# Feed-forward up projections as seven block products of sums, with the split of h behind them

## The reference, cut to what matters

```python
def swiglu(x, w_in, w_out):
    g, u = jnp.split(x @ w_in, 2, axis=-1)
    return (jax.nn.silu(g) * u) @ w_out

h = h + 0.5 * swiglu(rms_norm(h, ffn1_norm[i]), ffn1_w_in[i], ffn1_w_out[i])
```

## Time and profile before

| what | value |
| --- | --- |
| median of 3 runs | 2918.87 us (2911.94 to 2919.1) |
| the profiled execution, its own time | 2917.88 us |
| its span | 2916.1 us |
| PE busy | 2889.1 us, 99% |
| DVE, ACT, POOL busy | 39%, 38%, 44% |
| DMA | 267.5 MB, mean 92 GB/s |
| weights of the up parts | 220 units of 512 KB |

### The profile page before, as it was taken

The page is one execution under the profiler, slowest core; times in us unless marked ns, Lnnn a source line. Parts: engine busy times, 40 slices in busy tenths (PEclk is TensorE's granted clock), DMA queues, the critical chain, the costliest instruction groups (busy, mean ns, idle before and its releaser), DMA issues.

```text
span 2916.1 us, 36136 instructions
## 1 busy us (share of the span) xinstructions
PE 2889.1 (99%) x13036; PEld 2328.5 (80%) x13036; DVE 1122.8 (39%) x1659; ACT 1094.7 (38%) x1508; POOL 1285.4 (44%) x588
## 2 busy tenths in 40 slices
PE   8999999999999999999999999999999999999999
PEld 7888877888888888888888886765688888788887
DVE  4223157322312221135322216579788363432210
ACT  4232266333323322243323333556444344432321
POOL 4444444444444444443444443158632363244443
PEclk9999999999999999999999999999999999999999
DMA  4323322333333333332333322112222352233332
GB/s 153 100 90 104 96 87 80 101 94 93 94 101 94 101 98 91 99 110 87 94 101 102 92 89 87 52 51 65 87 73 66 94 150 68 65 94 101 94 93 80
DMA packets 80653, 267.50 MB, mean 92 GB/s; under 512 B 11168, under 2 KB 13216, under 8 KB 80560
## 3 DMA queue, kind: packets, MB, share of 16 engines
q1 hardware_dynamic: 77904, 262.01, 30.0%
q10 hardware_dynamic: 2656, 4.26, 0.5%
HBM read 263.09 MB, written 2.10 MB: 91 GB/s over the span
## 4 chain that ended last, share of the span: by engine, by line
PE 94%; DVE 3%; issue 1%; ACT 1%; POOL 0%; DMA 0%; ACTq 0%; SPq 0%; DVEq 0%; POOLq 0%
PE bank L437 28%; PE bank L439 27%; PE bank L438 27%; PE bank L509 1%; PE bank L511 1%; PE bank L510 1%; PE bank L2414 1%; PE bank L1142 1%; PE bank L1554 1%; PE bank L2152 0%; PE bank L1563 0%; PE bank L2132 0%; PE bank L1214 0%; PE bank L736 0%; DVE hq L2323 0%
## 5 line engine op out<-in xcount | busy, mean ns | idle before, releaser
L420 POOL TENSOR_TENSOR w_lo<-w_stage,w_hi 128x1024 fp32r<-128x1024 f32 (+1 forms) x448 | 1059.0, 2366 | 1408.0 <-ACT w_hi L394 1402.7
L437 PE MATMUL bank<-xg_hi,w_hi 128*128 128x512 f32 x2384 | 942.0, 395 | 1.6 <-POOL w_lo L432 1.2
L439 PE MATMUL bank<-xg_hi,w_lo 128*128 128x512 f32 x2384 | 928.3, 389 | 0.0
L438 PE MATMUL bank<-xg_lo,w_hi 128*128 128x512 f32 x2384 | 928.3, 389 | 0.0
L394 ACT ACTIVATE w_hi<-w_stage 128x1024 fp32r<-128x1024 f32 (+2 forms) x500 | 515.4, 1033 | 530.2 <-PE bank L439 487.5
L437 PEld LDWEIGHTS bank<-xg_hi,w_hi 128*128 128x128 f32 x2384 | 447.5, 188 | 122.8 <-issue 29.6
L438 PEld LDWEIGHTS bank<-xg_lo,w_hi 128*128 128x128 f32 x2384 | 447.7, 188 | 94.9 <-issue 4.1
L439 PEld LDWEIGHTS bank<-xg_hi,w_lo 128*128 128x128 f32 x2384 | 447.5, 188 | 94.3
L438 PE MATMUL bank<-h_lo,w_hi 128*128 128x512 f32 x880 | 342.3, 389 | 0.0
L437 PE MATMUL bank<-h_hi,w_hi 128*128 128x512 f32 x880 | 342.3, 389 | 0.0
L439 PE MATMUL bank<-h_hi,w_lo 128*128 128x512 f32 x880 | 342.3, 389 | 0.0
(11 more groups left out here) (474 smaller groups left out, 2995.5 us busy)
## 6 DMA issues: line engine op xcount, KB each, us to landing
w_stage<-w_up SPq DMA_DIRECT2D x220, 512.0 KB, 3.5
w_stage<-w_down SPq DMA_DIRECT2D x80, 512.0 KB, 3.5
w_stage<-merge SPq DMA_DIRECT2D x36, 512.0 KB, 3.6
w_stage<-w_down SPq DMA_DIRECT2D x40, 384.0 KB, 3.1
w_stage<-hg_qfg SPq DMA_DIRECT2D x12, 512.0 KB, 3.5
w_stage<-rec_r SPq DMA_DIRECT2D x8, 512.0 KB, 3.6
w_stage<-rec_y SPq DMA_DIRECT2D x8, 512.0 KB, 3.5
w_stage<-rec_out SPq DMA_DIRECT2D x8, 512.0 KB, 3.5
```

Source lines behind the costliest of these rows:

```text
L420: pool.tensor_tensor(w_lo[:, r, 0:w], w_stage[:, r, 0:w], f32(w_hi[:, r, 0:w]), ALU.subtract).then_inc(w_lo_ready, 1)
L437: pe.matmul(out, w_hi[:, r, c], hi, start=start, stop=False)
L438: pe.matmul(out, w_hi[:, r, c], lo, start=False, stop=False)
L439: return pe.matmul(out, w_lo[:, r, c], hi, start=False, stop=stop)
```

## The change

In each up projection, the first and the last body (four pairs) stay as they were on PE. The 18 pairs between are computed by blocks. The pair's two units are the rows of a 2 x 2 block matrix (W11, W12 in the unit of u, W21, W22 in the unit of g; the columns are the first and the second four tiles of x), and x is a 2 x 2 block matrix too (four tiles by 256 tokens). Seven products of blocks, each of 4 x 3 matmuls of 128 x 256, take the place of eight.

This needs sums. Once per part, DVE makes four sums of blocks of x (13 operations, `x_sums`), ACT their high and POOL their low parts (`x_high`, `x_low`). For each pair, ACT copies W21 into PSUM, DVE makes S1, S2 and S4 there, POOL makes S3; ACT writes the four high parts, DVE three low parts and POOL one. After the products, ACT copies M1, and DVE adds the blocks into the banks of u and g (five additions of 256 columns and one of 512). The banks 4 and 5 hold M5, M6 and M7, the banks 6 and 7 the sums of W.

The gate is handled in a new way: DVE multiplies g by `rstd` (`take_gate`), ACT takes silu, POOL multiplies the result by `rstd` (`scale_gate`), and DVE multiplies it with u straight from PSUM into `h_raw` (`product`). h is split only after the loop (`high` on ACT, `low` on DVE), because its place in memory holds the sums of x until then. SyncE's loads in the loop also wait for S4 of the pair that held the place before. Semaphores that are free by then are used twice, under new names.

The core of the diff:

```diff
+    xsum = place("xsum", [P, 4, 2, 4, HALF], F32R, at=work + 64)
+    s1_w = place("s1_w", [P, 2, T], F32R, at=work + 33 * KB)
+    s2_w = place("s2_w", [P, 2, T], F32R, at=work + 37 * KB)
+    u_add0 = place("u_add0", [P, T], at=work + 41 * KB)
+    u3 = place("u3", [P, HALF], at=work + 43 * KB)
+    xsum_f = place("xsum_f", [P, 5, 4, HALF], at=work + 68 * KB)
...
+            for k in range(4):
+                c = slice(k * P, (k + 1) * P)
+                pe.matmul(out, wh[:, c], xh[:, k, :], start=k == 0, stop=False)
+                pe.matmul(out, wh[:, c], xl[:, k, :], start=False, stop=False)
+                mm = pe.matmul(out, wl[:, c], xh[:, k, :], start=False, stop=k == 3)
+            return mm
...
+        def step(b, p):
+            n = pair_at(b, p)
+            pe.wait_ge(w_lo_ready, n * 2 + (U.base + 5))
+            pe.wait_ge(taken, n * 2 + (U.rbase + 1))
+            product(right(g_bank(p)), w_block(p, 0, 0), x_block(0, 0)).then_inc(block_mm, 1)
+            pe.wait_ge(taken, n * 2 + (U.rbase + 2))
+            product(left(u_bank(p)), w_block(p, 0, 1), x_block(1, 0)).then_inc(unit_used, 1)
+            pe.wait_ge(wsum_lo_ready, after_wsum_lo(i, "S1", n))
+            if first_pair(n):
+                pe.wait_ge(std_ready, q + 1)
+                pe.wait_ge(pool_lo_ready, after_pool_lo(i, 0) - 1)
+            else:
+                pe.wait_ge(block_add, n * 5 + (after_add(i, "g2", 0) - 5))
+            product(M5_OUT, (s1_w[:, 0], s1_w[:, 1]), x_sum(0)).then_inc(block_mm, 1)
+            pe.wait_ge(w_lo_ready, n * 2 + (U.base + 6))
+            pe.wait_ge(block_copied, n + (PAIRS * i + 1))
+            product(left(g_bank(p)), w_block(p, 1, 1), x_sum(3))
+            pe.wait_ge(pool_lo_ready, after_pool_lo(i, n))
+            product(M7_OUT, (s3_w[:, 0], s3_w[:, 1]), x_sum(2)).then_inc(block_mm, 1)
+            pe.wait_ge(wsum_lo_ready, after_wsum_lo(i, "S2", n))
+            product(M6_OUT, (s2_w[:, 0], s2_w[:, 1]), x_sum(1)).then_inc(block_mm, 1)
+            product(right(u_bank(p)), w_block(p, 1, 0), x_block(1, 1)).then_inc(unit_used, 1)
...
+        for u in range(RING):
+            project_unit(pe, U, U.bodies - 1, u, xg_hi, xg_lo, free=U.rbase + 4 * (U.bodies - 1) - 2 + 2 * (u // 2))
         def down(b):
             for m in range(4):
-                pe.wait_ge(taken, b * 4 + (L.rbase + m + 1 - RING))
+                pe.wait_ge(taken, b * 4 + (L.rbase + (m | 1) + 1 - RING))
                 for part in range(3):
                     u = 3 * m + part
                     k1 = min(8 * part + 8, KF)
                     pe.wait_ge(w_lo_ready, b * L.per + (L.base + u + 1))
-                    pe.wait_ge(h_lo_ready, KF * i + k1)
                     for k in range(8 * part, k1):
+                        if m == 0:
+                            pe.wait_ge(h_lo_ready, KF * i + k + 1)
                         mm = three_passes(pe, bank[m][:], u % RING, k - 8 * part, h_hi[:, k, :], h_lo[:, k, :],
                                           k == 0, k == KF - 1)
                     mm.then_inc(unit_used, 1)
...
+        def x_low(t):
+            pool.wait_ge(wsum_hi_ready, (4 * PAIRS + 8) * i + 4 + t + 1)
+            pool.tensor_tensor(xsum[:, t, 1], xsum_f[:, 1 + t], f32(xsum[:, t, 0]), ALU.subtract).then_inc(pool_lo_ready, 1)
...
+        def scale_gate(j):
+            pool.wait_ge(silu_done, j + (KF * i + 1))
+            pool.tensor_tensor(gbuf[:], gbuf[:], rstd[:], ALU.mult).then_inc(silu_scaled, 1)
+        def step(b, p):
+            n, b1, p1 = pair_at(b, p), b + p, 1 - p
+            row(b1, p1, 0)
+            scale_gate(n + 1)
+            s3(n + 1, p1)
+            row(b1, p1, 1)
+            s3_low(n + 1)
+        for u in range(RING):
+            plain(0, u)
+        x_low(0)
+        x_low(1)
+        s3(0, 0)
+        row(1, 0, 0)
+        x_low(2)
+        x_low(3)
+        row(1, 0, 1)
+        scale_gate(0)
+        s3_low(0)
...
+        step(last - 1, 0)
+        plain(last, 0)
+        scale_gate(KF - 4)
+        plain(last, 1)
+        plain(last, 2)
+        scale_gate(KF - 3)
+        plain(last, 3)
+        scale_gate(KF - 2)
+        scale_gate(KF - 1)
...
+        def wsum_high(name, n, p):
+            dst = {"S1": s1_w[:, 0], "S2": s2_w[:, 0], "S3": s3_w[:, 0], "S4": w_hi[:, 2 * p + 1, 0:T]}[name]
+            src = {"S1": S12_BANK, "S2": S12_BANK, "S3": s3_f, "S4": S4_BANK}[name]
+            if name == "S3":
+                act.wait_ge(s3_done, n + (PAIRS * i + 1))
+            else:
+                act.wait_ge(wsum_done, after_wsum(i, name, n))
+            if name != "S4" and not first_pair(n):
+                act.wait_ge(block_mm, n * 4 + (after_block(i, {"S1": "M5", "S2": "M6", "S3": "M7"}[name], 0) - 4))
+            act.activation(dst, src[:], ACT.Copy).then_inc(wsum_hi_ready, 1)
...
+        def step(b, p):
+            n, b1, p1 = pair_at(b, p), b + p, 1 - p
+            copy21(b1, p1, n + 1)
+            copy_m1(n, p)
+            row1(b1, p1)
+            silu(n + 1)
+            wsum_high("S1", n + 1, p1)
+            row2(b1, p1)
+            wsum_high("S4", n + 1, p1)
+            wsum_high("S3", n + 1, p1)
+            wsum_high("S2", n + 1, p1)
...
+        for k in range(4):
+            act.activation(xsum_f[:, 0, k, :], x[:, k, 0:HALF], ACT.Copy, scale=col(*gain(k))).then_inc(wsum_hi_ready, 1)
+        x_high(0)
+        x_high(1)
+        copy21(1, 0, 0)
+        row1(1, 0)
+        x_high(2)
+        x_high(3)
+        wsum_high("S1", 0, 0)
+        row2(1, 0)
+        silu(0)
+        for name in ("S4", "S3", "S2"):
+            wsum_high(name, 0, 0)
+        with act.Fori(1, U.bodies - 2) as b:
...
+        split_hi(act, U, last, 2)
+        split_hi(act, U, last, 3)
+        silu(KF - 3)
+        for j in range(6):
+            high(j)
+        split_hi(act, L, 0, 0)
+        for j in range(6, 12):
+            high(j)
+        split_hi(act, L, 0, 1)
+        silu(KF - 2)
+        for j in range(12, 18):
+            high(j)
+        split_hi(act, L, 0, 2)
+        for j in range(18, 21):
+            high(j)
+        silu(KF - 1)
+        high(KF - 1)
...
+        def x_sums():
+            for k in range(4):
+                dve.wait_ge(wsum_hi_ready, (4 * PAIRS + 8) * i + k + 1)
+                dve.scalar_tensor_tensor(xsum_f[:, 1, k, :], x[:, k, HALF:T], col(*gain(k)), xsum_f[:, 0, k, :],
+                                         ALU.mult, ALU.subtract).then_inc(xsum_done, 1)
+            dve.wait_ge(xsum_done, XSUMS * i + 4)
+            for k in range(4):
+                dve.scalar_tensor_tensor(xsum_f[:, 2, k, :], x[:, 4 + k, HALF:T], col(*gain(4 + k)), xsum_f[:, 1, k, :],
+                                         ALU.mult, ALU.subtract).then_inc(xsum_done, 1)
+            dve.wait_ge(xsum_done, XSUMS * i + 8)
+            dve.tensor_tensor(xsum_f[:, 3], xsum_f[:, 2], xsum_f[:, 0], ALU.subtract).then_inc(xsum_done, 1)
+            for k in range(4):
+                dve.scalar_tensor_tensor(xsum_f[:, 4, k, :], x[:, 4 + k, 0:HALF], col(*gain(4 + k)), xsum_f[:, 2, k, :],
+                                         ALU.mult, ALU.subtract).then_inc(xsum_done, 1)
...
+        def wsum(name, b, n, p):
+            w11, w12, w22 = w_stage[:, 2 * p, 0:T], w_stage[:, 2 * p, T:2 * T], w_stage[:, 2 * p + 1, T:2 * T]
+            if name == "S1":
+                dve.wait_ge(w21_copied, n + (PAIRS * i + 1))
+                ins = dve.tensor_tensor(S12_BANK[:], S12_BANK[:], w22, ALU.add)
+            elif name == "S2":
+                dve.wait_ge(w_loaded[2 * p], b * 16 + 16 * (U.base // RING + 1))
+                ins = dve.tensor_tensor(S12_BANK[:], S12_BANK[:], w11, ALU.subtract)
+            else:
+                dve.wait_ge(wsum_done, after_wsum(i, "S2", n))
+                ins = dve.tensor_tensor(S4_BANK[:], w12, S12_BANK[:], ALU.subtract)
+            ins.then_inc(wsum_done, 1)
...
+        def u2_sum(n, p):
+            dve.wait_ge(block_copied, n + (PAIRS * i + 1))
+            dve.wait_ge(block_mm, after_block(i, "M6", n))
+            dve.tensor_tensor(right(u_add(p)), M6_OUT, left(u_add(p)), ALU.add).then_inc(block_add, 1)
+        def other_sums(n, p):
+            dve.wait_ge(block_add, after_add(i, "U2", n))
+            dve.tensor_tensor(u3[:], M7_OUT, right(u_add(p)), ALU.add).then_inc(block_add, 1)
+            dve.tensor_tensor(right(u_add(p)), M5_OUT, right(u_add(p)), ALU.add).then_inc(block_add, 1)
+            dve.wait_ge(block_add, after_add(i, "U3", n))
+            dve.tensor_tensor(right(g_bank(p)), M5_OUT, u3[:], ALU.add).then_inc(block_add, 1)
+            dve.tensor_tensor(left(g_bank(p)), left(g_bank(p)), u3[:], ALU.add).then_inc(block_add, 1)
+            dve.wait_ge(unit_used, n * 2 + (U.base + 6))
+            dve.wait_ge(block_add, after_add(i, "u2", n))
+            dve.tensor_tensor(u_bank(p)[:], u_bank(p)[:], u_add(p)[:], ALU.add)
+            dve.wait_ge(block_add, after_add(i, "g1", n))
```

(49 more changed lines are left out.)

290 lines of the change are left out of this document (203 added, 87 removed).

## The result

The changed kernel takes 2938.64 us (median of 4 runs, 2937.39 to 2941.23), the kernel before 2916.57 beside it (2911.94 to 2919.1): 1.0081 times as long, interval 1.0069 to 1.0093. So it is slower by 0.8%, where the forecast was 1.6%; the profiled executions differ by 23.3 us (2939.4 less 2916.1). In the text TensorE is PE, VectorE DVE, ScalarE ACT and GpSimd POOL, as in the rows.

A forecast was written before the change was run, and what follows sets the result against it. The prediction took TensorE's matmul stream, busy 99% of 2916.1 us, as the bound. Its terms, -72 + 65 + 10 + 27.5 + 17 = +47.5 us on 2917.9 us, gave 2965 us, 1.6% slower, range 2905 to 3010.

The forecast's parts named there:

- steady pairs: In the up loop, 90 pairs take 10.08 us in place of 10.88 if nothing makes PE wait: -72 us.
- entering the loop: At each part's first changed pair, M1 waits for a gate queued behind DVE's sums, which POOL holds up: +65 us.
- fill behind it: After the loop is entered the pipeline must fill, about 2 us per part: +10 us (0 to 20).
- leaving the loop: After the last up matmul, PE waits for gate, silu, scaling and first down split, 5.5 us per part: +27.5 us.
- clock: PE runs at 1.2 GHz for some us after each of the ten waits: +17 us (0 to 34).
- a pair takes 84 x 0.120: In the steady loop, 84 matmuls of 256 columns at 0.120 us each make a pair of 10.08 us.
- second rival: The loop doesn't close in 10.08 us; PE waits 0.4 us in each of 85 pairs: 3000 us, chance 0.15.
- 11.7 us from the end of the reciprocal: At the loop's entry, the time until the first gate is taken if DVE's queued operations run alone: 11.7 us.
- first rival: At the loop's entry the sums of x aren't held up, so the start costs 10 us: 2906 us, chance 0.22.
- M2 waits for POOL's scaling, +1.5: Behind the loop's entry, M2 waits for POOL's scaling of the gate and DVE's product: +1.5 us.
- 1 at the start, where the other engines bound the first pairs anyway: Half clock after the wait at each up phase's start costs only 1 us, since other engines bound the first pairs.
- Third rival: 256-column matmuls run at 109 ns, so the other engines' loops hold the pair at 9.7 us: 2931 us, chance 0.05.

The follow-up runs named there:

- experiment 9: Changed kernel with the high and low parts of the x sums placed at a multiple of 2048 bytes, no longer 64 bytes behind one: 2949.03 us.
- experiment 10: Changed kernel with x, its high and low parts, the weights and all behind them moved on by 64 bytes, the x sums left in place: 2949.16 us.
- experiment 1: Changed kernel with POOL making the low parts of the first three down units before it scales the last gate: 2901.36 us.
- experiment 8: Kernel before the change with up units from each part's second body on multiplied in two halves of 256 columns instead of one of 512: 2978.52 us.
- experiment 2: Changed kernel with ACT's four copies of x ahead of its root and DVE's 13 sums of x ahead of its reciprocal: 2915.76 us.
- experiment 3: Changed kernel with the first gate taken right after the reciprocal, its silu and scaling moved forward, its product right after the sums of x: 2927.90 us.
- experiment 4: Experiment 2 with POOL scaling the first gate before the last two low parts of x, not behind them and a split: 2902.33 us.
- experiment 5: Changed kernel with down splits ahead of the last gate, sums of x early, and the loop's entry queued in the order PE asks: 2865.91 us.
- experiment 6: Experiment 5 with two of the four low parts of x made by DVE instead of POOL: 2854.09 us.
- experiment 11: Changed kernel with the weights' parts and all behind them moved on by 64 bytes, x and its high and low parts left in place: 2941.31 us.

## Why the prediction was right and wrong

The direction, the three places and, but for the fill, the mechanisms were right: time is won in the pairs, lost where the loop is entered and left, and again by the clock behind those waits. The size was twice too large. Four terms were too pessimistic, by 9 (the pace of the pairs), 9.5 (entering), 10 (the fill) and 2 us (leaving); the clock was 8 too low and hid some of that. By the steps of the sum, on the profiled executions:

| term | predicted | measured | from |
|---|---|---|---|
| steady pairs | -72 | -81 | 90 x (9.98 - 10.88) |
| entering the loop | +65 | +55.5 | waits before M1 |
| fill behind it | +10 | 0 | no wait between M1 and the end of the up phase |
| leaving the loop | +27.5 | +25.5 | waits before the first down matmul |
| clock | +17 | +25 | half of 27.3 + 22.3 |
| sum | +47.5 | +25 | 23.3 in the spans |

The 1.7 us between 25 and 23.3 are half of the 3.4 us at half clock that only the kernel before has, at 1814.7.

**Steady pairs.** The step "a pair takes 84 x 0.120" took its pace from operands that all lie alike. 48 of the 84 matmuls read the x sums, and these run at 117.9 ns by their place against the weights (experiments 9 and 10). 48 x 2.1 ns is 0.10 us per pair, 9 us in all. That the others keep up was right: there is no wait in the loop, so the second rival is false, though its margin of 0.2 us was real (DVE is busy for 7.5 of 10 us there).

**Entering the loop.** Right in kind: the first M1 is released by the gate, and POOL's turns hold up the sums. In part 2 they hold them up by 1.2 + 2.1 + 7.4 = 10.8 us (2.90, 3.82 and 9.08 against 1.67 for four), which is the 10.9 of the forecast; in part 1 by 9.4. Mis-sized was DVE's own work, "11.7 us from the end of the reciprocal", which is 10.5 (21.3 less 10.8), and PE came 12.2 us behind the reciprocal and not 11.65: 9.18 us of wait for 10.95. The first rival (no hold-up) is false.

**Fill.** The step "M2 waits for POOL's scaling, +1.5" failed. In part 2 the product ends at 572.51, and M2's first matmul starts at 572.60, one slow step of 0.21 us behind the last of M1 at 572.39: it did not wait. The slow clock that I priced by itself covers what I priced as fill: the two terms are one.

**Leaving the loop.** Right, 5.1 us for 5.5; removing it (experiment 1) gave 37.3 us, where the waits and half of their slow stretches are 36.7.

**Clock.** The step "1 at the start, where the other engines bound the first pairs anyway" was mis-sized. The starts cost 2.7 us each: PE is on the path there too, at once. The ends cost 2.2 each, for 2.5.

**Third rival.** False: no 256-column stream ran at 109 ns; the Trainium skill's gap for a single matmul (TensorE: Matmul & The Clock Gate, "Back-to-back issue gap") is not the pace of such a stream, as experiment 8 shows with 120.0.

## What to carry to other kernels

A change that shortens a saturated engine's stream by a few per cent can be decided at the two edges of its loop, as it was here. Write down, for each in-order queue, what stands ahead of the first and the last item that the saturated engine needs, and put it in the order in which that engine asks. When one wait goes, follow the next queue before you price the gain (experiments 2 and 3), and add something for the clock behind each wait of TensorE: it was 1.9 to 3.1 us behind the ten waits of 5 to 19 us here. Before you credit a gain to an edit, compare the granted clock in the stages that it doesn't touch (experiments 4 to 6).

## What the hardware did that I had not expected

- The pace of a matmul depends on where its moving operand lies against its weights. 256 columns: 120.0 ns with both at a multiple of 512 bytes or both 64 behind one, 117.7 to 117.9 with 64 bytes between them. In two parts of experiment 11 it was 113.5, with the same addresses. 512 columns: 226.7 without, 233.3 with. The cause is open; distances other than 64 bytes weren't tried.
- A wait of 4.05 us at the start of a part was followed by 3.2 us at half clock with PE busy (experiment 2), one of 0.8 us there by none (experiment 4). In experiment 5 the same wait of 1.9 us was followed by 3.4 us at half clock in part 4 and by none in parts 2, 3 and 5, so the length of a wait alone doesn't fix what follows it.
- In experiment 5 the clock is at half for 10.2 us from 1774.6 on, in a mixing stage of small matmuls that no edit touches. Experiment 11 has the same there (10.2 us from 1834.2 on) and the kernel before 3.4; the changed kernel and experiment 6 keep the full clock. Such a stretch costs some 5 us, and what decides on it is open.
